# Turning three of four x groups by VectorE blocks and DRAM scratches instead of on TensorE, between the first FFN and the attention layer

## What is computed

```
def reference(x, ...):
    for layer in range(DEPTH):
        h = rms_norm(x, mix_norm[layer])
        mix = even_mixer(h, ...) if layer % 2 == 0 else window_attention(h, w_qkv, ...)
        x = x + mix
        x = x + swiglu(rms_norm(x, ffn_norm[layer]), w_ffn_in[layer], w_ffn_out[layer])
    return rms_norm(x, final_norm)
```

## Time and profile before

| | before |
|---|---|
| median of three runs | 2005.01 us |
| lowest and highest run | 2004.62 and 2005.32 us |
| the profiled execution | 2005.5 us, of which span 2003.7 us |
| TensorE clock granted, mean over the span | 0.999 of full speed |
| TensorE matmul busy | 1993.1 us (99%) |
| VectorE busy | 1723.9 us (86%) |
| ScalarE busy | 1210.9 us (60%) |
| GpSimd busy | 170.7 us (9%) |
| DMA | 461.40 MB, mean 230 GB/s |

### The profile page before, as it was taken

The page is one execution under the profiler, slowest core; times in us unless marked ns, Lnnn a source line. Parts: engine busy times, 40 slices in busy tenths (PEclk is TensorE's granted clock), DMA queues, the critical chain, the costliest instruction groups (busy, mean ns, idle before and its releaser), DMA issues.

```text
span 2003.7 us, 24476 instructions
## 1 busy us (share of the span) xinstructions
PE 1993.1 (99%) x9206; PEld 1652.6 (82%) x9206; DVE 1723.9 (86%) x1640; ACT 1210.9 (60%) x1215; POOL 170.7 (9%) x216
## 2 busy tenths in 40 slices
PE   9999999999999999999999999999999999999998
PEld 7888888888888888888888887888888888888886
DVE  5666676789999999999996467789999999999995
ACT  6745555555656656656657466555656566566665
POOL 0000000100111101111100000100111101111010
PEclk9999999999999999999999999999999999999999
DMA  8755443867998888988877644676988889988886
GB/s 273 234 186 168 151 149 136 275 208 229 271 262 257 249 253 259 265 256 261 242 241 229 192 147 148 215 231 228 271 259 251 252 245 272 264 257 245 250 243 186
DMA packets 237187, 461.40 MB, mean 230 GB/s; under 512 B 16480, under 2 KB 21376, under 8 KB 236992
## 3 DMA queue, kind: packets, MB, share of 16 engines
q1 hardware_dynamic: 202832, 386.97, 58.1%
q0 software_dynamic: 30496, 69.22, 16.6%
q10 hardware_dynamic: 3792, 4.34, 0.7%
HBM read 401.10 MB, written 17.29 MB: 209 GB/s over the span
## 4 chain that ended last, share of the span: by engine, by line
PE 93%; DVE 4%; ACT 1%; DMA 1%; issue 1%; ACTq 0%; SPq 0%; DVEq 0%
PE ps L1790 60%; PE ps L1575 29%; PE ps L1681 1%; DVE w_lo L941 1%; DVE g_lo L1308 1%; DMA raw<-in_w_ab_in 1%; ACT junk L529 0%; DVE w_lo L1315 0%; PE ps L1601 0%; PE ps L1948 0%; PE ps L1923 0%; PE ps L1936 0%; ACT w_hi L486 0%; DVE w_sum L1296 0%; DMA x<-in_x 0%
## 5 line engine op out<-in xcount | busy, mean ns | idle before, releaser
L1308 DVE TENSOR_TENSOR g_lo<-g_raw,g_hi 128x2048 fp32r<-128x2048 f32 x240 | 545.8, 2287 | 6.5 <-ACT g_hi L740 0.5
L941 DVE TENSOR_TENSOR w_lo<-raw,w_hi 128x1024 fp32r<-128x1024 f32 x248 | 294.9, 1220 | 143.7 <-ACT w_hi L486 137.3
L731 ACT CAST g_hi<-g_raw 128x2048 fp32r<-128x2048 f32 x120 | 229.9, 1916 | 216.7 <-DVE g_raw L1282 208.0
L486 ACT ACTIVATE w_hi<-raw 128x1024 fp32r<-128x1024 f32 x248 | 254.3, 1056 | 142.8 <-DMA raw<-in_w_ab_in 52.2
L1575 PE MATMUL ps<-w_hi,xT_hi 128*128 128x512 f32 x672 | 264.4, 393 | 1.1 <-DVE w_lo L941 1.1
L1790 PE MATMUL ps<-g_hi,xT_hi 128*128 128x512 f32 x680 | 264.7, 389 | 0.1
L1790 PE MATMUL ps<-g_hi,xT_lo 128*128 128x512 f32 x680 | 264.5, 389 | 0.0
L740 ACT CAST g_hi<-g_raw 128x2048 fp32r<-128x2048 f32 x120 | 225.4, 1911 | 60.3 <-PE ps L1790 60.3
L1575 PE MATMUL ps<-w_hi,xT_lo 128*128 128x512 f32 x672 | 261.8, 390 | 0.0
L1575 PE MATMUL ps<-w_lo,xT_hi 128*128 128x512 f32 x672 | 261.6, 389 | 0.0
L1790 PE MATMUL ps<-g_hi,h0T_hi 128*128 128x512 f32 x640 | 249.2, 389 | 0.0
(11 more groups left out here) (226 smaller groups left out, 3139.1 us busy)
## 6 DMA issues: line engine op xcount, KB each, us to landing
g_raw<-in_w_ffn_in SPq DMA_DIRECT2D x320, 512.0 KB, 4.8
g_raw<-in_w_ffn_out SPq DMA_DIRECT2D x160, 512.0 KB, 4.8
raw<-in_w_ab_in SPq DMA_DIRECT2D x96, 512.0 KB, 4.7
x<-y POOLq DMA_DIRECT2D x80, 512.0 KB, 6.5
raw<-in_w_qkv SPq DMA_DIRECT2D x40, 512.0 KB, 4.7
raw<-in_w_ab_out SPq DMA_DIRECT2D x32, 512.0 KB, 4.7
raw<-in_w_ffn_in SPq DMA_DIRECT2D x32, 512.0 KB, 4.8
raw<-in_w_c_out SPq DMA_DIRECT2D x32, 512.0 KB, 5.2
```

The lines of the kernel that those rows point to most:

```text
L486: act.activation(w_hi[:, s, :], raw[:, s % RAWS, :], ACT.Copy).then_inc(hi_ready, 1)
L731: act.copy(dst[:, 0:4, :].rearrange("p s w -> p (s w)"), src[:, :, :].rearrange("p s w -> p (s w)")).then_inc(group_hi_ready, 1)
L941: dve.tensor_tensor(w_lo[:, s, :], raw[:, s % RAWS, :], w_hi[:, s, :], ALU.subtract).then_inc(lo_ready, 1)
L1308: ins = dve.tensor_tensor(lo_part[:, 0:4, :].rearrange("p s w -> p (s w)"), src[:, :, :].rearrange("p s w -> p (s w)"), hi_part[:, 0:4, :] ...
```

## The change

For phase 2, groups 0 to 2, the transposes of TensorE are taken out and the other way of turning is put in, with buffers, scratches (`x2_dram`, three of them) and semaphores of its own. The buffers `x2_blk` and `x2_rows` are two each, so group 2 uses those of group 0. Group 3 is turned on TensorE as before. TensorE runs Y 0 to Y 7 without a break; VectorE has `turn_x2(n)` behind each add and `x2_los(n)` later; ScalarE squares the groups earlier and has `x2_his(n)` between its splits; GpSimd has `carry_x2(n)` ahead of layer 1's carries.

```diff
+            def carry_x2(n):
+
+                pool.wait_ge(x2_turned, n + 1)
+                pool.dma_start(x2_dram[n], x2_blk[n % 2][:, :, :, :, :].rearrange("p j k t b -> p j (k t b)")).then_inc(x2_out[n], 16)
+                pool.wait_ge(x2_out[n], 16)
+                if n == 2:
+                    pool.wait_ge(xT_ready, 16 + 2)
+                for j in range(4):
+                    src = bass.AP(tensor=x2_dram[n].tensor, offset=x2_dram[n].offset + j * 256,
+                                  ap=[[1024, 32], [32 * 1024, 4], [1, 256]])
+                    pool.dma_start(x2_rows[n % 2][32 * j:32 * (j + 1), :, :, :, :].rearrange("p i k t b -> p i (k t b)"),
+                                   src).then_inc(x2_rows_in[n], 16)
+
             for layer in range(2):
+                if layer:
+                    for n in range(3):
+                        carry_x2(n)
                 for n in range(3):
                     carry_x(layer, n)
...
             Q = R_QKV
-            for g, (r, s, pair) in enumerate(((Q, 1, 0), (Q, 3, 1), (Q, 5, 2), (Q + 1, 0, 3))):
-                ahead(r, s)
-                xT_his(2, g, PAIR[pair])
+            def x2_his(n):
+
+                act.wait_ge(x2_rows_in[n], 64)
+                for b in range(2):
+                    for h in range(2):
+                        kk_ = 2 * b + h
+                        k = 4 * n + kk_
+                        ins = act.mul(xT_hi[:, k, :].rearrange("p (t i b) -> p t i b", t=NT, i=4),
+                                      x2_rows[n % 2][:, :, kk_, :, :].rearrange("p i t b -> p t i b"),
+                                      cols[:, COLS[2] + k:COLS[2] + k + 1])
+                    ins.then_inc(xh_ready, 1)
+
+            def square_added(g):
+
+                act.wait_ge(x_added, x_count(1, 1, g))
                 square_group(2, g)
+
+            ahead(Q, 1)
+            square_added(0)
+            ahead(Q, 3)
+            square_added(1)
+            x2_his(0)
+            ahead(Q, 5)
+            square_added(2)
+            x2_his(1)
+            ahead(Q, 7)
+            x2_his(2)
+            ahead(Q + 1, 0)
+            xT_his(2, 3, PAIR[3])
+            square_group(2, 3)
             ahead(Q + 1, 1)
             root(2)
...
+            def turn_x2(n):
+
+                dve.wait_ge(x_added, x_count(1, 1, n))
+                if n == 2:
+                    dve.wait_ge(x2_out[0], 16)
+                for t in range(NT):
+                    ins = dve.transpose(x2_blk[n % 2][:, :, :, t, :].rearrange("p j k b -> p k j b"), x[:, t, n * W:(n + 1) * W])
+                ins.then_inc(x2_turned, 1)
+
+            def x2_los(n):
+
+                for b in range(2):
+                    dve.wait_ge(xh_ready, 16 + 2 * n + b + 1)
+                    for h in range(2):
+                        kk_ = 2 * b + h
+                        k = 4 * n + kk_
+                        for t in range(NT):
+                            ts = slice(t * P, (t + 1) * P)
+                            ins = dve.scalar_tensor_tensor(
+                                out=xT_lo[:, k, ts].rearrange("p (i b) -> p i b", i=4), in0=x2_rows[n % 2][:, :, kk_, t, :],
+                                scalar=cols[:, COLS[2] + k:COLS[2] + k + 1],
+                                in1=xT_hi[:, k, ts].rearrange("p (i b) -> p i b", i=4),
+                                op0=ALU.mult, op1=ALU.subtract)
+                    ins.then_inc(xT_ready, 1)
+
             ahead(Y, 7)
             add_last(0, Y)
+            turn_x2(0)
             ahead(Q, 1)
-            xT_los(2, 0, PAIR[0])
             add_last(1, Y)
+            turn_x2(1)
             ahead(Q, 3)
             add_last(2, Y)
-            xT_los(2, 1, PAIR[1])
+            turn_x2(2)
+            x2_los(0)
             ahead(Q, 5)
             add_last(3, Y)
-            xT_los(2, 2, PAIR[2])
+            x2_los(1)
+            ahead(Q, 7)
+            x2_los(2)
             ahead(Q + 1, 0)
             xT_los(2, 3, PAIR[3])
...
             Y, Q = R_QKV - 1, R_QKV
-            down(Y, FB - 1, 0, 0, 4, *hT[1])
+            down(Y, FB - 1, 0, 0, 8, *hT[1])
             pe.wait_ge(y_copied, GROUPS * BLOCKS)
-            turn_x(2, 0, PAIR[0], x_count(1, 1, 0))
-            down(Y, FB - 1, 0, 4, 6, *hT[1])
-            turn_x(2, 1, PAIR[1], x_count(1, 1, 1))
-            down(Y, FB - 1, 0, 6, 8, *hT[1])
-            turn_x(2, 2, PAIR[2], x_count(1, 1, 2))
             pe.wait_ge(xT_ready, 16 + 2)
             fresh_round(Q, 16, {1: lambda: turn_x(2, 3, PAIR[3], x_count(1, 1, 3))})
```

More of the change, by code:

```diff
@@ L218, in trunk @@
         x_rows = [sb(f"x{i}_rows", [P, 4, 4, NT, 32], at=r1 + (36 + 4 * i) * KB) for i in range(2)]
+        x2_blk = [sb(f"x2{i}_blk", [P, 4, 4, NT, 32], at=bias_at + (8 + 4 * i) * KB) for i in range(2)]
+        x2_rows = [sb(f"x2{i}_rows", [P, 4, 4, NT, 32], at=bias_at + (16 + 18 * i) * KB) for i in range(2)]
         q_c = sb("q_c", [P, 2, NT, W], at=r1)
@@ L233, in trunk @@
         x_dram = [nc.dram_tensor(f"x{i}_dram", [P, 4, 8 * 32], F32, kind="Internal").ap() for i in range(2)]
+        x2_dram = [nc.dram_tensor(f"x2{i}_dram", [P, 4, 8 * 32], F32, kind="Internal").ap() for i in range(3)]
         ps = ctx.enter_context(nc.psum_tensor("ps", [P, 8, W], F32))
@@ L275, in trunk @@
         x_out, x_rows_in = [sem("x0_out"), sem("x1_out")], [sem("x0_rows_in"), sem("x1_rows_in")]
+        x2_turned = sem("x2_turned")
+        x2_out, x2_rows_in = [sem(f"x2{i}_out") for i in range(3)], [sem(f"x2{i}_rows_in") for i in range(3)]
         pair_landed = [sem(f"pair{i}_landed") for i in range(6)]
@@ L2026, in xt_count @@
 def xt_count(phase, g):
-    return (0, 8, 10, 18)[phase] + (2 * g if phase % 2 == 0 else 0)
+    return (0, 8, 10, 12)[phase] + (2 * g if phase == 0 else 0)
 def group_at(layer, f):
```

## The result

The changed kernel takes 2014.58 us, the median of six runs (2009.54 to 2017.1), against 2004.8 for the kernel before: ratio 1.0044, 95% interval 1.0033 to 1.0054. It is slower, where 2005.4 with a range of 2002.4 to 2010 was forecast. The kernel before spreads over 0.7 us, the changed one over 7.6. The profiled execution took 2014.76 us (span 2013.0, so 9.3 us more span).

The account below looks back on a forecast made before the run. TensorE was taken to bound the kernel. Sparing it three turns (2.63 us) against waits for the carries at Q 0 (1.4 us) and Q 4 (1.7 us) left Q 4 0.45 us late: 2005.4 us, range 2002.4 to 2010.

Parts of the forecast that it names:

- What bounds the kernel, and the gain: TensorE, busy 99% of the span, bounds; three turns of transposes removed before round Q save at most 2.63 us.
- Costed at nothing: VectorE's added 1.84 us a group, ScalarE's stops, later weight loads and 15 added DMAs were taken as hidden.
- The chain of the carries: GpSimd's writes and reads of groups 0 to 2 in one queue; Q 4 forecast to start 0.45 us late.
- i: Time from a group's first read issue to its last landing; taken as 7, 5.7 and 5.7 us, sum 18.4.
- the low end: Reads of groups 1 and 2 taken at 5.7 us, since SyncE would send at most two weight loads per stretch.
- the middle: Reads of group 0 taken at 7 us, within a range of 5.7 to 9.4.
- the half clock: TensorE at 1.2 GHz after standing still; a slow restart was priced at 1.85 us, only as a rival.
- the formula: Q 4 starts at 1078.1 + 2 x 1.6 + 2.15 plus the three read times; 0.45 us late for 18.4.
- the signs of being wrong: Last two read times over 7 us, no wait, matmul spacing behind a wait over 0.227 us, or a wait behind Q 6.
- Everything hidden: Rival: reads land fast enough that only small or no waits of TensorE remain; 2002.4 us, chance 0.16.
- Carries queue up: Rival: on GpSimd's queue reads are as slow as old carries, sum 26.8, Q 4 8.85 us late; 2013.9, chance 0.29.
- The clock: Rival: TensorE restarts slowly after standing still, costing 1.85 us; 2007.2 us, chance 0.06.

Follow-up runs that it names:

- x2_direct: Changed kernel without the carries: ScalarE and VectorE read the blocks VectorE transposed, in another data order; 2002.46 us, ratio 0.9987.
- x3_unused: Kernel before, TensorE still turning all groups, with VectorE's block transposes and the three carries run beside it, results unused; 2004.98 us, ratio 0.9998.
- x9_hold_next: Changed kernel, bias and Q + 1 loads held until group 2's reads land, group 3's split and add moved earlier; 2009.89 us, ratio 1.0023.
- x12_only12_hold: Changed kernel carrying only groups 1 and 2, loads from Q 6 held until group 2 lands, splits reordered; 2002.67 us, ratio 0.9990.
- x6_order: Changed kernel with GpSimd issuing write 1 before the reads of group 0; 2011.22 us, ratio 1.0031.
- x10_order_fill: x6_order with 26 idle matmuls ahead of TensorE's wait before Q 0; 2009.1 us, ratio 1.0021.
- x4_hold: Changed kernel, SyncE's loads of Q 4, Q 6, and bias with Q + 1 held until groups 0, 1 and 2 land; 2013.14 us, ratio 1.0039.
- x11_hold_reorder: x4_hold without the hold on bias and Q + 1, with x9_hold_next's order on ScalarE and VectorE; 2007.66 us, ratio 1.0011.
- x13_hold_late: Changed kernel, Q 4 and Q 5 loads held for group 0, later loads for group 2, splits as in x12_only12_hold; 2004.91 us, ratio 1.0000.
- x8_only12: Changed kernel with group 0 turned on TensorE again, only groups 1 and 2 carried; 2005.8 us, ratio 1.0004.
- after_again: The changed kernel unaltered, measured again on another occasion as yardstick; 2012.11 us, ratio 1.0034.
- x1_fill: Changed kernel with 20 idle matmuls ahead of TensorE's wait before Q 0 and 14 before Q 4; 2013.45 us, ratio 1.0038.
- x7_order_hold: x6_order with the held loads of x4_hold added; 2014.15 us, ratio 1.0044.

## Why the prediction was wrong

**What bounds the kernel, and the gain:** right. TensorE saved 2.63 us in sum; x2_direct measured 2.7.

**Costed at nothing:** right for VectorE, ScalarE and the added traffic (x2_direct, x3_unused), and no wait appeared behind Q 4 in the changed kernel.

**The chain of the carries:** the mechanism was right, its sizes were not, and this is the step that failed. Forecast and measured:

| step | forecast | measured |
|---|---|---|
| write 0 issued | 1074.5 | 1074.10 |
| reads 0 issued | 1078.1 | 1079.53 |
| group 0 landed (i) | 1085.1 (7) | 1088.33 (8.8) |
| reads 1 issued | 1086.7 | 1090.19 |
| group 1 landed (i) | 1092.4 (5.7) | 1094.84 (4.65) |
| reads 2 issued | 1094.0 | 1098.90 |
| group 2 landed (i) | 1099.7 (5.7) | 1106.86 (7.96) |
| Q 4 starts | 1101.85 | 1108.99 |

The sum of the three i was 21.4 and not 18.4: 3.0 of the 7.1 us by which Q 4 started later than forecast. The reason given for the low end was wrong for group 2: "SyncE ... sends at most two loads" held and was not enough, because two loads of 512 KB that go out among the reads (1099.1 and 1100.3) are beside an i of 8 and not 5; x9_hold_next, without them, has 4.66. For group 0 I took the middle, where the changed kernel's engines were at a share of 0.91 and i at the old carries' value. The other 4.1 us lie where I saw no unknown at all: in the writes. I priced write 0 at 3.6 us to the reads' issue; it took 5.4, and went out 0.4 earlier (1.4 in all). I had the reads follow 1.6 us behind the landing of the carry before; for group 1 that was 1.9, for group 2 it was 4.1. Write 2 is issued behind the reads of group 1, which landed so fast (2.3 us after its issue) that they hid little of its own time, and it shared the engines with Q + 1's loads (6.1 us to land, 3.4 in x9_hold_next).

The last term that failed is the half clock: the sum has nothing for it, only a rival of 0.06, and behind Q 4 it cost 1.7 us. With the measured i alone the formula gives 0.45 + 3.0 = 3.5 us late, 2008.5, which lies inside the range. The writes' 4.1 and the clock's 1.7 make it 9.3 us, the measured difference of the spans. The bounds held only the reads' time, so the range ended at 2010.

Of the signs of being wrong, two came: the last i was over 7 (the one before it was not), and the spacing behind a wait was wider than 0.227 us.

**Everything hidden (chance 0.16):** false for this kernel, nearly true for x12_only12_hold. The figures of the Trainium skill, DMA: Bandwidth & Descriptors, Anatomy of one DMA, give an estimate of 2.3 us for a read of 128 KB. Reads that went out with no weight load in flight came near it: those of group 1 landed 2.8 to 2.9 us after their issue. Those of group 0, with weight loads beside them, did not, at 4.9 to 7.1:

```profile
L479 POOL DMA_DIRECT2D x_rows<-x_dram x4: 553/558/592, 1079.5 to 1081.2; - x4
...
DMA to landing us min/median/max: 4.9/5.8/7.1
...
L479 POOL DMA_DIRECT2D x_rows<-x_dram x4: 551/556/560, 1090.2 to 1092.0; - x4
...
DMA to landing us min/median/max: 2.8/2.9/2.9
```

**Carries queue up (0.29):** this is what happened, and its time, 2013.9, was close, partly by luck: the i were smaller than it had them (21.4 against 26.8), and the writes and the clock made up the difference. Given the numbers it deserved more than the forecast: all six carries of the kernel before spoke for it, and for the low i only an argument. Their i go from 7.2 to 9.5; the prediction's "no i in the trace is under 8.1" overlooks layer 1's second (issued at 1285.29, landed at 1292.5), but even that is over the 5.7 it took.

**The clock (0.06):** it happened as well, twice. I had it as a rival to the others, where it is a consequence of any long wait; 1.85 us as its price was right (1.7 in the profile, 2.1 between x6_order and x10_order_fill). The Trainium skill says in TensorE: Matmul & The Clock Gate, HAM oscillation, that idle gaps between bursts of matmuls put the clock to 1.2 GHz. The trace agrees: 0.50 in the 4 us from 1090, behind the gap of 4.8 us.

## What to carry to other kernels

A transfer that is late can cost three times: the wait, the slow clock behind it, and the next transfer that stands behind it in the queue. So when work moves off the engine that bounds, each hand-over of the new path needs its own upper bound, the writes as well as the reads, taken with the traffic that runs beside it. Before giving the idea up, look at who else uses the engines in that stretch: delaying weight loads that weren't due (and the splits that go with them) turned 1.0004 into 0.9990 for two groups, and 1.0044 into 1.0000 for three. And a slow stretch ahead of a second wait costs nothing; count only what lies behind the last one.

## What the runs showed of the hardware

- Landing of four 128 KB reads from GpSimd, first issue to last landing, at this place and with each write behind the reads before it: 4.5 to 5.4 us with no 512 KB load of SyncE in flight as they went out and none issued among them (x12_only12_hold, groups 1 and 2 of x9_hold_next, group 0 of x4_hold and x11_hold_reorder, groups 0 and 2 of x13_hold_late); 5.2 to 7.4 where such loads were in flight but none was issued among the reads (groups 1 and 2 of x4_hold and x11_hold_reorder, group 0 of x3_unused at the low end, group 1 of x8_only12 at the high end); 7.3 to 9.3 where one or two were (groups 0 and 2 of the changed kernel, after_again and x1_fill, group 0 of x9_hold_next). The total traffic doesn't say it: at a DMA share of 0.69 over the stretch i was still 7.96, at 0.63 in x4_hold it was 4.9. These are readings of one profile each, and the moment of issue was not varied by itself.
- In x6_order, where GpSimd issues the reads of two groups behind each other, the eighth of them went out 4.25 us behind the seventh, at 1090.30, though the program has no wait between them. The last read of group 0 had landed at 1089.96. In x10_order_fill and x7_order_hold it went out 0.35 us behind that landing as well. What holds it back no run shows, but it delays write 2, which stands behind it.
- The clock fell behind waits of 4.8, 3.3 and, in x11_hold_reorder, 2.2 us (0.64 in the 4 us from 1104). It stayed at 1.00 behind the 1.6 us of x8_only12 and the 1.9 us of x7_order_hold at Q 0. It fell while TensorE stood still (0.89 in 1086 to 1090) or, at the second wait, a few matmuls after the restart: the first behind 1108.99 start 0.34 and 0.24 us apart, the later ones 0.43.
